# Output projection of a fused decoder layer by pairs of token tiles in seven products, with the sums of w_out made in the second branch

## The reference, cut to what matters

```python
proj = jnp.einsum('btd,de->bte', rms_norm(x, norm_w), w_in) + b_in        # 7 gates, q, k, v, z, ...
branch_a = jnp.einsum('bte,ed->btd', attn * jax.nn.silu(a_z), w_branch_attn)
branch_m = jnp.einsum('bte,ed->btd', h_m, w_branch_mlstm)
merged = jax.nn.sigmoid(g_attn) * branch_a + jax.nn.sigmoid(g_mlstm) * branch_m
x = x + jnp.einsum('btd,de->bte', merged, w_out)
return rms_norm(x, final_norm_w)
```

## Time and profile before

| what | value |
|---|---|
| median of 3 runs | 1136.5 us (1135.45 to 1136.57) |
| time of the profiled execution | 1134.48 us |
| its span, first to last instruction | 1132.7 us |
| mean granted TensorE clock | 0.999 |
| PE busy | 1110.4 us (98%), 5411 matmuls |
| DVE busy | 737.1 us (65%) |
| ACT busy | 466.4 us (41%) |
| POOL busy | 603.3 us (53%) |

### The profile page before, as it was taken

How to read it: one execution, slowest core, us unless ns; L and a number is a source line. 1 busy time by engine, 2 the same in 40 slices (tenths; PEclk the granted TensorE clock), 3 DMA queues, 4 the chain that set the end, 5 groups by cost and what they waited for, 6 DMA issues and landing times.

```text
span 1132.7 us, 16545 instructions
## 1 busy us (share of the span) xinstructions
PE 1110.4 (98%) x5411; PEld 886.4 (78%) x5411; DVE 737.1 (65%) x1201; ACT 466.4 (41%) x1112; POOL 603.3 (53%) x416
## 2 busy tenths in 40 slices
PE   5999999999999999999999999999999999999997
PEld 5787777777777778888888888888887888888886
DVE  5866887887878886576756675667677322655333
ACT  6544433534434443455445454536464212112221
POOL 5477455465564478557945795569452343541000
PEclk9999999999999999999999999999999999999999
DMA  7135133142151141113311231123119334432222
GB/s 227 44 96 87 38 93 93 29 122 64 37 157 39 28 131 38 38 47 86 92 38 39 83 102 37 37 83 97 44 48 361 112 93 161 140 108 74 93 74 93
DMA packets 108513, 99.20 MB, mean 88 GB/s; under 512 B 7164, under 2 KB 93560, under 8 KB 108456
## 3 DMA queue, kind: packets, MB, share of 16 engines
q1 hardware_dynamic: 98936, 69.11, 20.9%
q10 hardware_dynamic: 9520, 29.36, 8.2%
HBM read 76.31 MB, written 22.15 MB: 87 GB/s over the span
## 4 chain that ended last, share of the span: by engine, by line
PE 82%; DVE 8%; ACT 3%; DVEq 3%; issue 2%; ACTq 1%; DMA 0%; SPq 0%
PE ps L928 43%; PE ps L1157 15%; PE ps L841 3%; PE ps L1204 3%; PE ps L1205 3%; PE ps L1209 3%; PE ps L1015 2%; PE ps L1131 1%; PE ps L1115 1%; PE ps L1119 1%; PE ps L1128 1%; DVE v L2190 1%; PE ps L1057 1%; DVE row_max L1960 1%; PE ps L1064 1%
## 5 line engine op out<-in xcount | busy, mean ns | idle before, releaser
L753 POOL TENSOR_TENSOR ring_lo<-w,ring_hi 128x512 fp32r<-128x512 f32 x128 | 179.8, 1423 | 134.6 <-ACT ring_hi L1263 134.5
L753 POOL TENSOR_TENSOR ring_lo<-t,ring_hi 128x512 fp32r<-128x512 f32 x96 | 136.3, 1426 | 142.7 <-ACT ring_hi L1263 142.7
L928 PE MATMUL ps<-s_hi,ring_hi 128*128 128x512 f32 x512 | 203.5, 397 | 0.0
L928 PE MATMUL ps<-s_lo,ring_hi 128*128 128x512 f32 x512 | 202.7, 396 | 0.0
L928 PE MATMUL ps<-s_hi,ring_lo 128*128 128x512 f32 x512 | 202.0, 394 | 0.0
L928 PE MATMUL ps<-h_hi,ring_hi 128*128 128x512 f32 x384 | 151.9, 396 | 0.0
L928 PE MATMUL ps<-h_hi,ring_lo 128*128 128x512 f32 x384 | 151.9, 396 | 0.0
L928 PE MATMUL ps<-h_lo,ring_hi 128*128 128x512 f32 x384 | 151.4, 394 | 0.0
L1263 ACT ACTIVATE ring_hi<-w 128x512 fp32r<-128x512 f32 x128 | 75.7, 620 | 93.7 <-PE ps L928 79.6
L928 PEld LDWEIGHTS ps<-s_hi,ring_hi 128*128 128x128 f32 x512 | 96.2, 188 | 22.2 <-issue 3.1
L928 PEld LDWEIGHTS ps<-s_hi,ring_lo 128*128 128x128 f32 x512 | 96.2, 188 | 21.7 <-issue 2.6
(11 more groups left out here) (288 smaller groups left out, 2196.9 us busy)
## 6 DMA issues: line engine op xcount, KB each, us to landing
w<-in_w_in SPq DMA_DIRECT2D x128, 256.0 KB, 3.0
xs<-in_x SPq DMA_DIRECT2D x8, 512.0 KB, 6.4
ga_scratch<-ev ACTq DMA_DIRECT2D x4, 1024.0 KB, 4.8
u_scratch<-silu_z ACTq DMA_DIRECT2D x8, 512.0 KB, 3.3
gm_scratch<-ev ACTq DMA_DIRECT2D x4, 1024.0 KB, 4.8
w_raw<-in_w_branch_attn SPq DMA_DIRECT2D x8, 512.0 KB, 3.8
u_a_f<-u_scratch SPq DMA_DIRECT2D x4, 1024.0 KB, 7.7
ev<-ga_scratch ACTq DMA_DIRECT2D x8, 512.0 KB, 3.5
```

Source lines behind the costliest of these rows:

```text
L753: return nc.gpsimd.tensor_tensor(flat(lo[:]), flat(raw_or_sum[:]), flat(hi[:]).bitcast(F32), ALU.subtract)
L928: mm = nc.tensor.matmul(ps[:, bank, :], w[:, k, :], h[:, k, :], start=(m == 0), stop=(m == PRODUCT - 1))
```

## The change

The output projection takes two token tiles at a time (`OPAIRS`, 4 pairs). `merged` for a pair is cut into four blocks of 512 features by 128 tokens (`merged_part`), `w_out` into four of 512x512, and a pair is made in seven products of 12 matmuls (`output_pair`): 84 where there were 96.

Sums of weights. `o11`, `o12`, `o22` are blocks of `w_out`; `o_s1` to `o_s4` are sums of blocks. All of `w_out` is loaded at the start of the second branch. DVE makes s1 and s3 ahead of tile n = 2 and s2 and s4 ahead of n = 4. s1, s3 and s4 are stored to a scratch in memory (`keep_sum`) and loaded again (`f_again`) when the last tile has left the room of `UM` (`um_free`). ACT makes the high parts, DVE the low parts (`output_high`, `output_low`, `again_high`).

Sums of tokens. For each pair POOL makes four sums (`o_t1` to `o_t4`) and two low parts, ACT seven high parts and a copy of the first product, DVE five low parts. The results are gathered in `ev` and `x_more` by DVE (`half_of` and four additions), in the order in which the products end, and scaled and stored as before. PSUM banks alternate between pairs (`O_BANKS`).

```diff
+            def output_weights():
+                sp.wait_ge(tile_done, BM)
+                for half, dst in ((0, f_o11), (0, f_o21), (1, f_o22), (1, f_o12)):
+                    first = BANK if dst in (f_o21, f_o22) else 0
+                    sp.dma_start(dst[:], wo_rows[:, KH * half:KH * half + KH, first:first + BANK]).then_inc(wo_in, 16)
+            for i in range(KT // 2):
                 weights(BM + 2 * i, [(0, wbm_cols, 2 * P * i), (1, wbm_cols, P + 2 * P * i)])
+                if i == 0:
+                    output_weights()
+                if i == 1:
+                    keep_sum(1, 1, f_s1)
+                    keep_sum(0, 2, f_s3)
+                if i == 2:
+                    keep_sum(2, 4, f_s4)
...
+            for o in range(OPAIRS):
...
+                pool.wait_ge(merged_ready, KH)
+                if o:
+                    pool.wait_ge(merged_rest, 1)
+                    pool.wait_ge(w5_ready, i)
+                sub(o_t1[:], w12_o, w11_o).then_inc(sum_made, 1)
+                if o:
+                    pool.drain()
+                    sub(o_t2[:], w22_o, o_t1[:]).then_inc(sum_made, 1)
+                pool.wait_ge(w1_hi, i + 1)
+                sub(o_ring[0][1][:], w11_o, o_ring[0][0][:].bitcast(F32)).then_inc(w1_ready, 1)
...
+                pool.wait_ge(w6_hi, i + 1)
+                sub(o_ring[1][1][:], o_t2[:], o_ring[1][0][:].bitcast(F32)).then_inc(w6_ready, 1)
+                if o:
+                    pool.wait_ge(w7_ready, i)
...
+                sub(o_t3[:], w22_o, w12_o).then_inc(sum_made, 1)
+                if o:
+                    pool.wait_ge(w4_ready, i)
+                sub(o_t4[:], w21_o, o_t2[:]).then_inc(sum_made, 1)
...
+            def output_pair(o):
...
+                pe.wait_ge(w7_ready, i + 1)
...
+                terms(bank_d, o_ring[3], o_s3, 0, PRODUCT).then_inc(p7_done, 1)
+                pe.wait_ge(w4_ready, i + 1)
+                pe.wait_ge(a_copied, i + 1)
+                terms(bank_a, o_ring[0], o22, 0, PRODUCT).then_inc(p4_done, 1)
+                pe.wait_ge(w5_ready, i + 1)
+                pe.wait_ge(b_out, i + 1)
...
+                terms(bank_b, o_ring[1], o_s1, 0, PRODUCT).then_inc(p5_done, 1)
+                pe.wait_ge(w3_ready, i + 1)
+                pe.wait_ge(c11_out, i + 1)
...
+                terms(bank_c, o_ring[4], o_s4, 0, PRODUCT).then_inc(p3_done, 1)
...
+            for o in range(OPAIRS):
+                last = o == OPAIRS - 1
+                act.wait_ge(p1_done, WPAIRS + o + 1)
+                if o:
+                    act.wait_ge(y_out[0], 16 * o)
+                A(ev[:, 0, 0:BANK], ps[:, O_BANKS[o % 2][0], :], ACT.Copy, scale=0.5).then_inc(a_copied, 1)
...
+                if o:
+                    o_low_4(o)
+                dve.wait_ge(a_copied, i + 1)
+                dve.wait_ge(p6_done, i + 1)
+                if o:
+                    dve.wait_ge(y_out[1], 16 * o)
+                half_of(bank_b, ev_part(1, 0), ev_part(0, 0)).then_inc(b_out, 1)
...
+                o_low_5(o)
+                dve.wait_ge(x_in[0], 16 * (o + 2))
+                V.tensor_tensor(ev_part(0, 0), ev_part(0, 0), x_part(0, 0), ALU.add)
+                dve.drain()
+                dve.wait_ge(p2_done, i + 1)
+                half_of(bank_c, ev_part(0, 0), ev_part(0, 0)).then_inc(c11_out, 1)
...
+                V.tensor_tensor(ev_part(1, 0), ev_part(1, 0), x_part(1, 0), ALU.add)
+                if not last:
+                    o_low_2(o + 1)
+                scaled(o, 0)
+                dve.wait_ge(p3_done, i + 1)
+                half_of(bank_c, ev_part(1, 0), ev_part(1, 0)).then_inc(c12_out, 1)
+                if not last:
+                    o_low_7(o + 1)
+                scaled(o, 1)
+                if not last:
+                    o_low_3(o + 1)
```

More of the change, by code:

```diff
@@ L416, in build @@
         gate_tanh = sem("gate_tanh")
[L417 removed]
+        wo_in = sem("wo_in")
+        wo_sum = sem("wo_sum")
+        wo_stored = sem("wo_stored")
+        um_free = sem("um_free")
+        wo_again = [sem(f"wo_again{n}") for n in range(3)]
         wo_hi_ready = sem("wo_hi_ready")
@@ L433, in build, with merged_part @@
         sp_passed = sem("sp_passed")
-        mt_hi = [w_hi[slot(BO + s)][:] for s in range(2)]
-        mt_lo = [w_lo[slot(BO + s)][:] for s in range(2)]
+        def merged_part(half, o, j):
+            n = 2 * o + j
+            return merged[:, KH * half:KH * half + KH, n * P:(n + 1) * P]
         fnw = w_raw[0][:].rearrange("p k n -> p (k n)")
@@ L660, in _ @@
+            for n in range(3):
+                sp.wait_ge(um_free, n + 1)
+                sp.dma_start(f_again[n][:], scr_s[n]).then_inc(wo_again[n], 16)
+            sp.wait_ge(tile_done, BO)
             for j in range(2):
                 sp.dma_start(x_more[:, j, :], x_rows[:, j, :]).then_inc(x_in[j], 16)
[L663 to L674, removed]
+            for o in range(OPAIRS):
+                last = o == OPAIRS - 1
@@ L1144, in _, with branch @@
             ended(pe, PAIRS, mlstm_step)
-            def branch(t, s, part, first=None):
+            def branch(t, s, part, first=None, freed=False):
                 pe.wait_ge(w_split, t + 1)
@@ L1178, in branch_m_step @@
                 branch(BM + 2 * i, 1, um_part, None if later(i) else um_landed)
[L1179 to L1211, removed]
@@ L1216, in _ @@
+            for o in range(OPAIRS):
+                output_pair(o)
         @block.scalar
@@ L1701, in _ @@
             ended(act, KT // 2, branch_a_step)
[L1704 to L1712, removed]
-                    act.wait_ge(wo_in[j], 16 * (i + 1))
-                    A(UA[:, ds(i, 1), 0, j, :], UA_f[:, ds(i, 1), 1, j, :], ACT.Copy).then_inc(wo_hi_ready, 1)
-                    gate_tanh_of(j, KT // 2 + i + 1)
-                    if last and j == 1:
-                        act.wait_ge(merged_ready, KT - 1)
-                        act.wait_ge(tile_done, BO - 1)
-                        A(mt_hi[0][:, 0:KT - 1, :], merged[:, 0:KT - 1, 0:P], ACT.Copy).then_inc(mt_hi_ready, 1)
@@ new lines, in scaled @@
+            def scaled(o, j):
+                r = rstd[:, j:j + 1]
+                dve.wait_ge(res_sumsq, 4 * o + 2 * j + 2)
+                V.tensor_tensor(r, sumsq[:, 2 * j:2 * j + 1], sumsq[:, 2 * j + 1:2 * j + 2], ALU.add)
+                dve.drain()
+                V.tensor_scalar(r, r, 1.0 / D, EPS, ALU.mult, ALU.add).then_inc(res_var, 1)
+                dve.wait_ge(res_root, 2 * o + j + 1)
+                V.reciprocal(r, r)
+                dve.drain()
+                for part in (slice(0, BANK), slice(BANK, D)) if o == OPAIRS - 1 and j == 1 else (slice(0, D),):
+                    V.scalar_tensor_tensor(ev[:, j, part], ev[:, j, part], r, fnw[:, part], ALU.mult, ALU.mult)\
+                        .then_inc(y_ready, 1)
```

379 lines of the change are left out of this document (260 added, 119 removed).

## The result

| what | before | changed |
|---|---|---|
| median | 1135.6 us | 1137.5 us |
| ratio, 95% interval | | 1.0017 (1.0010 to 1.0024) |
| span of the profiled execution | 1132.7 us | 1135.2 us |

Both medians are of 20 executions; one of the changed kernel's took 1575.8 us at a granted clock of 0.66 and is left out of the ratio. The forecast's sum started from 1136.5, the median of three executions; twenty give 1135.6.

A forecast was written before the change was run, and what follows sets the result against it. PE bounds the kernel, but DVE's cycle would then set the pairs: matmuls -10.9, PE's gaps +18.2, tail +2.7, second branch +0.3 make +10.3 on 1134.5, plus 2.0 to the median: 1146.8 us; 8-in-10 range 1129 to 1152.

The forecast's parts named there:

- Matmuls, -10.9: Output projection on PE: 384 matmuls become 336, 48 x 0.2267 us saved if PE never waits.
- DVE's own work of a pair, 14.8: DVE in one output pair: evictions, low parts, additions, drains, norms and scalings sum to 14.8 us within PE's 19.04.
- for store and root: One DVE pair: 2.7 us for store and root, added to 14.8 of work and 6.0 of waits.
- Taking turns: DVE and POOL at SBUF: they alternate by whole instructions, not sharing bandwidth; a two-element operation takes 0.16 or up to 1.24 us.
- the five waits: One DVE pair: two additions, o_low_2 and the norm's two small operations wait for POOL, 6.0 us together, bounds 0 and 7.5.
- A store lands 3.3 us after issue: Row store that the next pair's first eviction waits for: lands 3.3 us after issue, so DVE stands some 2.2 us.
- The pair, 23.5: Output projection: eviction b to the next pair's b takes 23.5 us on DVE, so PE waits 4.5 us each.
- rival B: No change: two to three of five waits fall, a pair takes 20.4 us, 1136.3 us in all; chance 0.10.
- First pair, 4.8 of waits: PE's waits for late low parts and s4, plus the second pair starting 0.4 late: 23.8 us for 19.04.
- The tail, +2.7: End of last pair: DVE scales row 0 first and reaches product 3's eviction 2.7 us late, then the chain as before.
- Second branch, +0.3: Weight loads and POOL splits of tiles 17 and 19 nearly in time, tile 15 costing nothing: +0.3 us, between 0 and 6.
- rival C: Worse: splits of tiles 17 and 19 come 3 us late each, +6 on the sum, 1152.8 us; chance 0.10.

The follow-up runs named there:

- e1: Changed kernel with POOL's six operations in pairs 1 to 3 narrowed to 8 of 128 tokens per block, leaving out work: 1130.15 us.
- e8: Changed kernel with each of POOL's six operations in pairs 1 to 3 done twice, same result: 1151.1 us.
- e4: Changed kernel with the norm's two small DVE operations made one, second sum as per-partition scalar, epsilon as the root's bias: 1134.6 us.
- e7: Changed kernel with, in the last pair, the last PSUM eviction moved ahead of row 0's scaling: 1137.2 us.
- e6: Changed kernel with row 1 scaled into a buffer of its own and the norm's two small operations made one: 1131.3 us.

## Why the prediction was wrong in size

The mechanism held, and so did the sign; two terms of the pair were too large. Point by point, in the order of the sum:

- **Matmuls, -10.9.** Right: starts within a product are 0.23 apart at a clock of 1.00.
- **DVE's own work of a pair, 14.8.** Right. Measured: 21.0, less 4.6 of waits and 1.5 of the store, is 14.9, with the idle time for the root in it. In the forecast some of that idle time stood in the 2.7 "for store and root" as well.
- **Taking turns.** Right in kind. Shown by the 128x1 sum of 1.25 us and by e1, where the longer durations are gone; in e8 a second sum takes 1.24. The Trainium skill (SBUF — State Buffer, "SBUF: two separate sides") says that the pair of ports which DVE and GpSimd share is held for a whole instruction, and the trace agrees: 0.69 becomes 1.70, and 0.16 becomes 1.25.
- **"I take 6.0" for the five waits: the step that failed first.** Four fell as written, at 1.01, 1.09, 1.08 and 1.10 where I had 1.1, 1.25, 1.25 and 1.25; with 0.28 on a scaling they make 4.6. The fifth, the norm's second small operation, was put at 1.1 and is 0. It reads one tensor in SBUF, and I had classed it by its size and neighbours, not by its operands: my row for "an operation of two elements per partition" was one of two tensors. All eight took 153 to 155 ns, the three with POOL's operation under way from before their start to after their end like the other five. So of the 1.4 us per pair by which the 6.0 was too much, the fifth is 1.1; the four are 0.6 shorter, and the scaling's 0.3 goes the other way. The Trainium skill (SBUF — State Buffer, "Who interferes with whom") says that a DVE instruction with at most one SBUF input, outside the modes that use two ports, does not contend with GpSimd. The 0.15 agrees, and so does e4, which turned the first into a one-tensor form as well; in which mode an operation of one element runs, no run here shows.
- **"A store lands 3.3 us after issue": the second.** It took 2.6:

```profile
out<-ev SPq DMA_DIRECT2D x7, 512.0 KB, 2.6
```

I had used the median of the kernel before, and that mixes two kinds. There the seven took 6.2, 3.3, 4.6, 2.6, 4.8, 2.6 and 2.6 us: the 6.2, 4.6 and 4.8 were issued 0.4 to 0.6 us behind a load of `x_more`, the others 4.5 us and more behind one. In the changed kernel no store stands so close behind a load: the one that b waits for is issued 3.0 us behind, and took 2.6 each time. That is what the traces show; no run moved a load. So DVE stood 1.5 us. From the scaling of row 1 to b it is 2.8 where the forecast has 3.5: 0.7 per pair.
- **The pair, 23.5.** It is 21.0: 1.4 from the waits, 0.7 from the store, the other 0.4 from smaller steps. Three pairs make 7.5 of the 7.8 us by which the sum was off; PE's waits in the last three pairs say much the same, 6.1 us for 13.4. 21.0 lies between rival B's 20.4 and the forecast. The time is nearer to B's 1136.3 than to any other, but B had two or three waits fall, and four fell.
- **First pair, 4.8 of waits**, 4.4 of them inside it. Measured 0.34 ahead of product 2, 1.5 ahead of 7 and 0.9 for s4, with 0.2 to 0.3 around each: 3.5. The places are right. The DVE part of 2048 elements took 3.16, 3.39 and 2.62 beside POOL, which I had at 2.3. The 0.4 of the second pair is 1.4, ahead of its product 6. All gaps of PE in the stage are 10.2, forecast 18.2.
- **The tail, +2.7.** PE ends at 1126.5, the span at 1135.2: 8.7 for 6.5, so +2.2. Right within 0.5; e7's order saves 0.4 of it at most.
- **Second branch, +0.3, with tiles 17 and 19 as the risk.** Tile 17's split ended at 995.2, wanted at 996.2, and 19's at 1017.7, wanted at 1018.2: rival C did not come. The sentence that failed is that tile 15 costs nothing: its weights landed at 969.2, not 966, behind 4 MB that took this long:

```profile
w_raw<-in_w_branch_mlstm SPq DMA_DIRECT2D x8, 512.0 KB, 7.3
...
f_o<-in_w_out SPq DMA_DIRECT2D x4, 1024.0 KB, 9.7
```

PE then waited 0.5. The stage begins 1040.0 for 1039.1, of which 0.3 stood before this branch.
- **The sum.** -10.9 + 10.2 + 2.2 + 0.9 (start of the stage) = +2.4, and the spans differ by 2.5.

That the result is almost "no change" is no sign that the waits did not fall; 10.9 us of matmuls were saved and 10.2 given back in waits of PE. e6 shows what becomes of them when two of the causes are taken away: 1131.3 us.

## What to carry to other kernels

Before an idle engine gets work, list each neighbour operation by its operands, not its size: here a DVE operation of one element with two tensors in SBUF stood for a whole POOL operation, and one with a single tensor for none. The cheap repair is in the form (a second operand as a per-partition scalar) and in the place of the result (a buffer of its own for what a store still reads): two edits, worth 6.2 us together by the medians. Price a saved matmul only after stepping the slower engine through one whole cycle, and a term of each cycle by the number of cycles.

## What the runs showed of the hardware

- A 128x1 `tensor_tensor` took up to 1.25 us beside POOL, a 128x1 `tensor_scalar` 0.15, and with the second value as a per-partition scalar in SBUF 0.20, each three times with POOL's operation under way.
- The taking of turns lengthens POOL's side too: 128x512 in 1.75 us for 1.29, and 3.3 behind a DVE operation of 2048 elements.
- A store of 512 KB issued 0.4 to 0.6 us behind a load of 512 KB in the same queue landed in 4.6 to 6.2 us (three times in the kernel before); one issued 3 us or more behind a load landed in 2.6 to 3.3, in both kernels.
- After PE had stood idle for 3.3 to 4.4 us (e8) its step went from 0.227 to 0.427 us (granted clock from its upper to its lower level) for 8 to 13 matmuls. Waits of 0.3 to 1.5 us, nine of them in the changed kernel's stage, did nothing of the kind.
